# A second attention with keys on partitions: column maxima and sums by GpSimd in place of turned probabilities

## What is computed

```python
def _attention(q, k, v):
    ...
        s = jnp.einsum('bqhgd,bkhd->bhgqk', qi, k, preferred_element_type=jnp.float32)
        w = jax.nn.softmax(s, axis=-1).astype(v.dtype)
        return jnp.einsum('bhgqk,bkhd->bqhgd', w, v)
...
    q = _rope(_rmsnorm(_heads(p, OFF_Q, N_Q_HEADS), q_norm_g[l]), cos, sin) * q_scale
    attn = _attention(q, jnp.concatenate([k, kc], axis=1), jnp.concatenate([v, vc], axis=1))
...
    y_a = (attn * jax.nn.silu(z_a)) @ w_pa
```

## Time and profile before

| quantity | value |
|---|---|
| median of three runs | 2207.98 us |
| span of the profiled execution | 2206.3 us |
| TensorE matmul busy | 2197.4 us, 100% |
| VectorE busy | 1509.1 us, 68% |
| ScalarE busy | 1066.9 us, 48% |
| GpSimd busy | 63.1 us, 3% |
| mean granted TensorE clock | 0.999 |
| HBM | 215 GB/s over the span |

### The profile page before, as it was taken

How to read it: one execution, slowest core, us unless ns; L and a number is a source line. 1 busy time by engine, 2 the same in 40 slices (tenths; PEclk the granted TensorE clock), 3 DMA queues, 4 the chain that set the end, 5 groups by cost and what they waited for, 6 DMA issues and landing times.

```text
span 2206.3 us, 37987 instructions
## 1 busy us (share of the span) xinstructions
PE 2197.4 (100%) x16122; PEld 2068.7 (94%) x16122; DVE 1509.1 (68%) x1910; ACT 1066.9 (48%) x1418; POOL 63.1 (3%) x72
## 2 busy tenths in 40 slices
PE   9999999999999999999999999999999999999998
PEld 9999999999999889989988988998889999999987
DVE  7789588888889657544554555555766656577776
ACT  5444445544444546444443543444656555444443
POOL 1000000000000000000000000000100000010001
PEclk9999999999999999999999999999999999999999
DMA  8876676788787755656656666656664445678784
GB/s 275 241 225 209 192 247 221 228 281 258 256 278 264 241 182 182 195 194 194 192 195 195 183 202 203 197 186 207 235 196 148 135 144 172 216 264 294 251 281 156
DMA packets 248034, 475.00 MB, mean 215 GB/s; under 512 B 21526, under 2 KB 26000, under 8 KB 247096
## 3 DMA queue, kind: packets, MB, share of 16 engines
q1 hardware_dynamic: 243032, 454.40, 64.7%
q0 software_dynamic: 4832, 18.16, 2.5%
HBM read 468.30 MB, written 5.78 MB: 215 GB/s over the span
## 4 chain that ended last, share of the span: by engine, by line
PE 99%; issue 0%; DVE 0%; ACT 0%; POOLq 0%; POOL 0%; DVEq 0%
PE ps L888 21%; PE ps L889 21%; PE ps L890 21%; PE ps L881 11%; PE ps L882 11%; PE ps L883 11%; PE ps L805 1%; PE ps L705 1%; PE ps L794 0%; PE ps L674 0%; PE ps L902 0%; PE ps L717 0%; PE ps L784 0%; PE ps L785 0%; PE ps L783 0%
## 5 line engine op out<-in xcount | busy, mean ns | idle before, releaser
L888 PE MATMUL ps<-op0h,whiW 128*128 128x256 f32 x3376 | 936.8, 277 | 0.0
L890 PE MATMUL ps<-op0h,wloW 128*128 128x256 f32 x3376 | 932.3, 276 | 0.0
L889 PE MATMUL ps<-op0l,whiW 128*128 128x256 f32 x3376 | 932.2, 276 | 0.0
L1279 DVE TENSOR_TENSOR wloW<-raw,whiW 128x1024 fp32r<-128x1024 f32 (+1 forms) x503 | 611.0, 1227 | 339.0 <-ACT whiW L935 336.9
L935 ACT ACTIVATE whiW<-raw 128x1024 fp32r<-128x1024 f32 (+1 forms) x504 | 529.0, 1058 | 581.1 <-PE ps L890 482.8
L888 PEld LDWEIGHTS ps<-op0h,whiW 128*128 128x128 f32 x3376 | 633.7, 188 | 2.2 <-issue 1.6
L889 PEld LDWEIGHTS ps<-op0l,whiW 128*128 128x128 f32 x3376 | 633.8, 188 | 0.5
L890 PEld LDWEIGHTS ps<-op0h,wloW 128*128 128x128 f32 x3376 | 633.7, 188 | 0.0
L1279 DVE TENSOR_TENSOR wloT<-raw,whiT 128x1024 fp32r<-128x1024 f32 (+1 forms) x264 | 317.4, 1211 | 249.5 <-ACT whiT L935 248.0
L935 ACT ACTIVATE whiT<-raw 128x1024 fp32r<-128x1024 f32 (+1 forms) x264 | 273.7, 1046 | 291.0 <-PE ps L883 243.0
L881 PE MATMUL ps<-whiT,op1h 128*128 128x512 f32 x640 | 249.2, 389 | 0.0
(11 more groups left out here) (308 smaller groups left out, 2070.2 us busy)
## 6 DMA issues: line engine op xcount, KB each, us to landing
raw<-in_w_in SPq DMA_DIRECT2D x256, 512.0 KB, 4.4
raw<-in_w_up SPq DMA_DIRECT2D x128, 512.0 KB, 3.7
raw<-in_w_down SPq DMA_DIRECT2D x128, 512.0 KB, 4.0
raw<-in_w_ada SPq DMA_DIRECT2D x96, 512.0 KB, 4.7
raw<-in_w_gate SPq DMA_DIRECT2D x96, 512.0 KB, 4.8
raw<-in_w_out SPq DMA_DIRECT2D x64, 512.0 KB, 5.1
raw<-in_w_branch SPq DMA_DIRECT2D x48, 512.0 KB, 4.9
raw<-in_w_proj_a SPq DMA_DIRECT2D x24, 512.0 KB, 5.7
```

The costliest lines, as they stand in the source:

```text
L888: pe.matmul(o, wh, xh[:, ka, :], start=first and m % 2 == 0, stop=False, skip_group_check=True)
L889: pe.matmul(o, wh, xl[:, ka, :], start=False, stop=False, skip_group_check=True)
L890: mm = pe.matmul(o, wl, xh[:, ka, :], start=False, stop=last, skip_group_check=True)
L1279: v.tensor_tensor(wlo[job.mode][q % NSPL][:, :, 0:job.n], x, h.bitcast(F32), ALU.subtract).then_inc(s_lo, 1)
```

## The change

Scores are computed the other way round: 128 keys are stationary, the 256 queries of a head move, so the scores stand in four tiles of 128 keys by 256 queries. ScalarE copies them to a buffer `keyed[h % 2]` (128x1024, in place of tmp0 to tmp3). VectorE takes the maximum of the four tiles (128x256), GpSimd all-reduces the maxima of a pair of heads over partitions (`peaks2`, 128x512), VectorE subtracts them, ScalarE takes the exponential. `values2` reads these unnormalised values directly, with 256 moving columns. GpSimd adds the four tiles of each head and all-reduces the sums (`totals2`); VectorE takes the reciprocal of 128x512 and multiplies it with the gates (`softmax2_share`), and gates the values with that. Both heads' values go to bank 4. `turn2` and `softmax2_scale` are gone. The pairs stand 11, 11, 11, 17 and 11 chunks apart. `TURN_QK` names other banks for the turning of queries and keys.

```diff
+TURN_QK = ((6, 7), (5, 7), (5, 7), (5, 7), (5, 4))
...
-        heads2 = [of["za0"].first + 6, of["qq1"].first + 5, of["za1"].end, of["zb"].first + 1, of["ga0"].first + 3, of["ga0"].first + 10]
+        pairs2 = [of["za0"].first + i for i in (6, 17, 28, 39, 56, 67)]
         for i in range(6):
-            q = heads2[i]
+            q = pairs2[i]
             for h in (2 * i, 2 * i + 1):
                 side(pe_at, q, "scores2", h)
+                side(act_at, q + 1, "scores2", h)
                 side(dve_at, q + 1, "softmax2_max", h)
-                side(act_at, q + 1, "softmax2_exp", h)
-                side(dve_at, q + 1, "softmax2_scale", h)
-                side(pe_at, q + 3, "turn2", h)
-                side(act_at, q + 4, "turn2", h)
+                side(dve_at, q + 4, "softmax2_less", h)
+                side(act_at, q + 5, "softmax2_exp", h)
                 side(pe_at, q + 6, "values2", h)
-                side(dve_at, q + 7, "values2", h)
-                side(act_at, q + 7, "values2", h)
+            side(dve_at, q + 9, "softmax2_share", i)
+            for h in (2 * i, 2 * i + 1):
+                side(dve_at, q + 9, "values2", h)
+                side(act_at, q + 9, "values2", h)
...
+            def peaks2(i):
+                pool.wait_ge(s_max2, 2 * i + 2)
+                pool.partition_all_reduce(peak[:, :, :], peak[:, :, :], 128, bass.bass_isa.ReduceOp.max).then_inc(s_peak2, 1)
+
+            def totals2(i):
+                if i:
+                    pool.wait_ge(s_atv, 2 * i)
+                for e in range(2):
+                    p, o = keyed[e], total[:, e, :]
+                    pool.wait_ge(s_exp2, 2 * i + e + 1)
+                    pool.tensor_tensor(o, p[:, 0, :], p[:, 1, :], ALU.add).then_inc(s_sum2, 1)
+                    for st in (2, 3):
+                        pool.wait_ge(s_sum2, 6 * i + 3 * e + st - 1)
+                        pool.tensor_tensor(o, o, p[:, st, :], ALU.add).then_inc(s_sum2, 1)
+                pool.wait_ge(s_sum2, 6 * i + 6)
+                pool.partition_all_reduce(total[:, :, :], total[:, :, :], 128, bass.bass_isa.ReduceOp.add).then_inc(s_total2, 1)
...
-            for name in ("k", "qq0", "qq1", "qq2"):
-                rstd(name, 0)
-                rstd(name, 1)
+            rstd("k", 0)
+            rstd("k", 1)
+            rstd("qq0", 0)
+            rstd("qq0", 1)
+            peaks2(0)
+            totals2(0)
+            rstd("qq1", 0)
+            rstd("qq1", 1)
+            for i in range(1, 4):
+                peaks2(i)
+                totals2(i)
+            rstd("qq2", 0)
+            rstd("qq2", 1)
+            for i in range(4, 6):
+                peaks2(i)
+                totals2(i)
...
             def scores2(h):
...
                 if h >= 2:
-                    pe.wait_ge(s_att, h - 1)
-                    pe.wait_ge(s_trr2, 2 * h - 2)
...
+                    pe.wait_ge(s_scr2, h - 1)
+                    if e == 0:
+                        pe.wait_ge(s_atv, h)
+                qh, ql = qt[:, h, :], qtl[h // 4][:, h % 4, :]
+                for st in range(4):
+                    keys, ps = slice(128 * (st % 2), 128 * (st % 2) + 128), bank[4 + 2 * e + st // 2][:, 256 * (st % 2):256 * (st % 2) + 256]
+                    kh, kl = ((ktx, ktxl), (ktch, ktcl))[st // 2]
+                    pe.matmul(ps, kh[:, kv, keys], qh, start=True, stop=False)
+                    pe.matmul(ps, kh[:, kv, keys], ql, start=False, stop=False)
+                    mm = pe.matmul(ps, kl[:, kv, keys], qh, start=False, stop=True)
+                mm.then_inc(s_sc2, 1)
...
+                pe.wait_ge(s_exp2, h + 1)
+                for st in range(4):
+                    vv = vx if st < 2 else vc
+                    mm = pe.matmul(bank[4][:, 256 * e:256 * e + 256], vv[:, st % 2, 128 * kv:128 * kv + 128], keyed[e][:, st, :],
+                                   start=st == 0, stop=st == 3)
...
+            def scores2(h):
+                e = h % 2
+                if h >= 2:
+                    act.wait_ge(s_att, h - 1)
+                act.wait_ge(s_sc2, h + 1)
+                for i in range(2):
+                    op = act.activation(keyed[e][:, 2 * i:2 * i + 2, :], half(bank[4 + 2 * e + i]), ACT.Copy)
+                op.then_inc(s_scr2, 1)
+
             def softmax2_exp(h):
...
+                p = keyed[h % 2]
+                act.wait_ge(s_less2, h + 1)
+                act.activation(p[:, :, :], p[:, :, :], ACT.Exp, scale=ATT_SCALE).then_inc(s_exp2, 1)
...
             def softmax2_max(h):
...
+                v.wait_ge(s_scr2, h + 1)
+                v.tensor_reduce(peak[:, e, :], keyed[e][:, :, :].rearrange("p s t -> p t s"), AX, ALU.max).then_inc(s_max2, 1)
+
+            def softmax2_less(h):
+                e, p = h % 2, keyed[h % 2]
+                v.wait_ge(s_peak2, h // 2 + 1)
+                v.tensor_tensor(p[:, :, :], p[:, :, :], peak[:, e, :].unsqueeze(1).broadcast_to([128, 4, 256]), ALU.subtract).then_inc(s_less2, 1)
+
+            def softmax2_share(i):
...
+                v.wait_ge(s_total2, i + 1)
+                v.reciprocal(total[:, :, :], total[:, :, :]).then_inc(own.sem, own.up())
+                v.wait_ge(own.sem, own.n)
+                v.tensor_tensor(total[:, :, :], total[:, :, :], zs[:, 2 * i:2 * i + 2, :], ALU.mult).then_inc(s_share2, 1)
+                v.wait_ge(s_share2, i + 1)
...
             def values2(h):
...
                 v.wait_ge(s_av2, h + 1)
-                v.tensor_tensor(tm[:, 0:256], bank[4 + 2 * (h % 2)][:, 0:256], zs[:, h, :], ALU.mult).then_inc(s_atv, 1)
+                v.tensor_tensor(x, bank[4][:, 256 * e:256 * e + 256], total[:, e, :], ALU.mult).then_inc(s_atv, 1)
```

More of the change, by code:

```diff
@@ L380, in program @@
         cdt = bg("cdt", [128, 2, 128], 60)
+        keyed = [at(f"keyed{e}", [128, 4, 256], tmp_at + 4096 * e) for e in range(2)]
+        peak, total = at("peak", [128, 2, 256], tmp_at + 10240), bg("total", [128, 2, 256], 69)
         rot = [bg(f"rot{i}", [128, 512], 61 + 2 * i) for i in range(4)]
@@ L797, in values2 @@
+                mm.then_inc(s_sc2, 1)
             def values2(h):
                 e, kv = h % 2, h // 3
[L799 to L806, removed]
+                if h == 0:
+                    pe.wait_ge(s_pair[of["vx"].pair], of["vx"].after)
@@ L1034, in split_kc @@
                 act.activation(ktch, ktc[:, :, :], ACT.Copy).then_inc(s_kch, 1)
-            def softmax2_exp(h):
[L1037 to L1050, removed]
+            def scores2(h):
[6 more added lines that the diff above has]
+                op.then_inc(s_scr2, 1)
+            def softmax2_exp(h):
+                p = keyed[h % 2]
+                act.wait_ge(s_less2, h + 1)
+                act.activation(p[:, :, :], p[:, :, :], ACT.Exp, scale=ATT_SCALE).then_inc(s_exp2, 1)
             def values2(h):
                 act.wait_ge(s_atv, h + 1)
-                act.activation(op1h[:, h, :], tmp[4 + h % 2][:, 0:256], ACT.Copy).then_inc(s_ahi, 1)
+                act.activation(op1h[:, h, :], keyed[h % 2][:, 0, :], ACT.Copy).then_inc(s_ahi, 1)
             def fourier_t(g):
@@ L1205, in ep_gate2 @@
                     act.wait_ge(s_qkt, 10)
+                    if which == "b" and c == 1:
+                        act.wait_ge(s_atv, 12)
                 for m in range(4):
@@ L1544, in softmax2_max @@
             def softmax2_max(h):
[L1545 to L1550, removed]
+                e = h % 2
+                v.wait_ge(s_scr2, h + 1)
[5 more added lines that the diff above has]
+            def softmax2_share(i):
+                job = of[f"za{i // 2}"]
+                if i % 2 == 0:
+                    v.wait_ge(s_pair[job.pair], job.after)
+                v.wait_ge(s_total2, i + 1)
[3 more added lines that the diff above has]
+                v.wait_ge(s_share2, i + 1)
             def turn_qk(s, tt):
@@ L1560, in split_kc @@
                 v.tensor_tensor(ktcl[:, :, :], ktc[:, :, :], ktch.bitcast(F32), ALU.subtract).then_inc(s_kcl, 1)
[L1562 to L1568, removed]
-            def values2(h):
[L1571 to L1578, removed]
+            def values2(h):
+                e = h % 2
+                x = keyed[e][:, 0, :]
                 v.wait_ge(s_av2, h + 1)
-                v.tensor_tensor(tm[:, 0:256], bank[4 + 2 * (h % 2)][:, 0:256], zs[:, h, :], ALU.mult).then_inc(s_atv, 1)
+                v.tensor_tensor(x, bank[4][:, 256 * e:256 * e + 256], total[:, e, :], ALU.mult).then_inc(s_atv, 1)
                 v.wait_ge(s_ahi, h + 1)
-                v.tensor_tensor(op1l[:, h, :], tm[:, 0:256], op1h[:, h, :].bitcast(F32), ALU.subtract).then_inc(s_att, 1)
+                v.tensor_tensor(op1l[:, h, :], x, op1h[:, h, :].bitcast(F32), ALU.subtract).then_inc(s_att, 1)
             def fourier_d(g):
```

47 lines of the change are left out of this document (17 added, 30 removed).

## The result

The changed kernel takes 2253.97 us, the median of four runs (2250.46 to 2254.76), where the kernel before takes 2208.02: ratio 1.0204, 95% interval 1.0192 to 1.0217, slower by 46 us. The execution that was profiled is the fastest of the four, 2250.46 us, with a span of 2248.5 us, 42.2 more than the span before.

What follows compares the result with a forecast made beforehand. TensorE, busy practically the whole span, was taken as the bound. Waits of 3 x 6.2 + 6.4 + 5.0 + 11.4 + 14 = 55.4 us minus 11.3 removed make +44.1 on 2207.98: 2252 us, range 2206 to 2280.

Steps and rivals of the forecast that it cites:

- What goes away: TensorE: transposes of probabilities gone, 10.5 us, value matmuls 0.8 us less, scores cost the same; gain 11.3 us without waits.
- Maxima: VectorE, start of a pair's chain: maximum over 1024 values, 2 x 0.68 us; a strided read could cost twice that.
- All-reduce: GpSimd, 128x512, for a pair's maxima and again for its sums: mean 3.7 us each.
- Way back: GpSimd: changing its code from the all-reduce to ordinary adds, 8.4 us, hidden in a plain pair with 1 us of cover.
- Way forth: GpSimd: changing its code to the all-reduce's between additions and the all-reduce of sums, 8.4 us, bounds 0 and 9.4.
- rival 2: Cheap change of GpSimd's code, dear reciprocal: 21 us of waits minus 11.3, 2218 us; chance 0.13.
- Reciprocal: VectorE, 512 columns between all-reduced sums and gating: taken as 5.0 us, between 0.49 and 5.6.
- The sum of waits: TensorE: 6.2 us after pairs 0, 2 and 4, 6.4 at pair 5, 5.0 and 11.4 at pair 1, 14 near qq2; 55.4.
- Pair 1: rstd of qq1 between GpSimd's all-reduces delays pair 1's maxima all-reduce to 14 us behind its scores; pair 2's scores wait 11.4 us.
- late weights of chunks 19 to 21: Scaling and rotating of qq1 hold up these weights and the exponentials: 5.0 us of TensorE waiting.
- rival 3: TensorE's clock falls too, in waits of 6 us and more: 2.6 us for each of seven, 2270 us; chance 0.13.
- Rival 1: All hidden, faster: free change to the all-reduce's code, reciprocal near 0.5 us, gating within 33.5 us; 2196.7 us; chance 0.17.

Runs made afterwards that it cites:

- switch_after_adds: adds_on_vector plus one single-column GpSimd addition per pair, placed behind VectorE's six additions and before the all-reduce of the sums: 2250.25 us, ratio 1.0191.
- adds_on_vector: Changed kernel with the six additions of each pair moved from GpSimd to VectorE: 2213.25 us, ratio 1.0024 to the kernel before.
- no_reciprocal: Changed kernel with the reciprocal of 128x512 left out, gates multiplied with the sums themselves: 2224.2 us, ratio 1.0075 to the kernel before.
- adds_spread_v7: adds_spread with the value matmuls of pair 5 one chunk later: 2204.11 us, ratio 0.9984 to the kernel before.
- adds_spread: adds_on_vector with maxima by three comparisons and gating at q + 8, 8, 8, 11, 9 and 13 for the six pairs: 2205.24 us, ratio 0.9987.
- late_share: Changed kernel with reciprocal, gating and low part of pairs 3 and 5 at position q+12 instead of q+9: 2244.67 us, ratio 1.0165.

## Why the prediction was right, and where its terms were off

The mechanism was read right: each pair's chain through GpSimd and VectorE is longer than TensorE's slack. The time, 2254 against 2252 us, is nearer than the terms were, by luck. Step by step:

- **What goes away** was right. The value matmuls of a pair take 3.45 us, scores keep their 0.120 us, the transposes are gone.
- **Maxima** were too cheap. The strided reduction of 128x1024 takes 2.02 us, not 1.4; the upper bound had it (twice). For the four pairs whose additions waited for the exponentials it did not count. For pairs 1 and 3 it did: there the additions waited for the way back, which starts behind the all-reduce of the maxima, and two heads are some 1.2 us of that chain.
- **All-reduce** of the maxima: 1.8 to 2.7 us, mean 2.38, instead of 3.7; of the sums 3.29.
- **Way back** 7.0 to 8.4 us where it is exposed, as predicted. The six additions took 5.6 to 6.5 us with hand-overs instead of 4.8.
- **Way forth** was the term known least, 0 to 9.4, taken as 8.4. It is 6.3 on the mean. The choice of the nearest row over 0 made most of the forecast's loss: with 0, rival 2 still had the kernel slower, by 10 us instead of 44. switch_after_adds shows that it was the right mechanism. The 6 us of the Trainium skill, GPSIMD Engine Reference, "Instruction dispatch", are nearer to this term.
- **Reciprocal** 3.35 us. I took 5.0, too long. The estimate from the Trainium skill (VectorE: DVE Perf Modes, "First, the fixed hardware budget") was 4.3, too long as well.
- **The sum of waits** is therefore 38.2 us and not 55.4. Plain pairs 3.4, 4.8 and 3.1 where I had 6.2 each, pair 5 5.0 and 0.9 before its values where I had 6.4, pair 1 6.5 where I had 16.4. At qq2 14.5 against 14: the order (scaling queued behind the rstd behind the sums, the reciprocal behind the rotation) was read right, but the number is partly luck. Pair 3's all-reduce of the maxima started 9.5 us behind its scores where I had 3, and the shorter all-reduces, changes of code and reciprocal gave that back.
- **Pair 1** is the step whose reading failed, not only its size. I had the code ready for its maxima 12 us behind its scores, 55 us behind pair 0's; the rstds of qq1 were through at 1699.0, some 5 us earlier than I had, and the way forth is 2 us shorter. So its all-reduce waited for VectorE's maxima, 10.97 us, and not for "issue". The late weights of chunks 19 to 21 do not show either in the changed kernel, where TensorE came out of the wait at half its clock; in adds_on_vector, where it came there at the full clock, they do, with 2.2 us in two gaps.
- **The clock** was a rival (3), priced at 18 us and left out of the sum. It happened in each of the six waits above 3 us, where the rival had spoken of 6 us and more, and cost some 14 us; in adds_on_vector even a wait of 1.9 us had 3.4 us of lower clock behind it. I had the waits 17 us too long and the clock at nothing, 14 us too short, and that these two errors cancelled is luck. Forecast and rival 3 together are what took place.

Rival 1 (all hidden) needed a free way forth and a reciprocal of 0.5 us; no_reciprocal, which comes near the second (no reciprocal at all), still lost 16 us, and rival 1 is out. Rival 2 needed a free way forth; adds_on_vector is near what it described, at 2213 us against its 2218.

## What to carry to other kernels

Before a step is put on GpSimd, count how often its queue goes from an all-reduce to ordinary instructions and back: here 7 to 9 us one way and about 6 us the other, hidden where it can run beside another engine's work, paid in full where it starts behind the last thing it waits for. One single-column addition per pair cost 31 us more in the wrong place than in the right one. Where TensorE had never waited, 38 us of waits cost another 14 us at the lower clock here, while the waits of 1.1 to 1.5 us in adds_spread_v7 cost none (in adds_spread two of 1.5 us, 2.6 us apart, still had 3.4 us of lower clock behind them). So a chain should be shorter than its slack, not about as long.

## What the runs showed that I had not expected

The reciprocal of 128x512 takes 3.35 us, 6.5 ns a column, 3346 to 3355 ns in its six cases.

All-reduces of 128x512 are not of one length: 1.8, 2.7 or 4.9 us for the maxima. In the changed kernel pair 1's took 2.66 us, and in late_share, where everything up to there is the same program and it started equally long, 0.14 us, behind VectorE's maxima, 4.93 us:

```profile
1710.09 4.93 POOL L558 PARTITION_ALL_REDUCE peak<-peak  x1 [10.96 <-DVE peak L1567]
...
1726.52 3.28 POOL L569 TENSOR_TENSOR total<-total,keyed 128x256 f32<-128x256 f32 x2
1736.62 3.25 POOL L571 PARTITION_ALL_REDUCE total<-total  x1 [6.82 <-issue]
```

Beside it VectorE ran three low parts, which read two operands in SBUF, first in the changed kernel, then in late_share:

```profile
1709.73 4.33 DVE L1300 TENSOR_TENSOR wloW<-raw,whiW 128x1024 fp32r<-128x1024 f32 x3
1709.87 3.48 DVE L1300 TENSOR_TENSOR wloW<-raw,whiW 128x1024 fp32r<-128x1024 f32 x3
```

One side pays each time. In all 11 traces with this all-reduce it is one of these two pairs of lengths: in six VectorE takes 4.33 us and the all-reduce 2.66, in five VectorE some 3.5 us and the all-reduce 4.93. Likewise two additions took 3.28 us in late_share and 1.56 in the changed kernel, beside the low parts too. The Trainium skill, SBUF — State Buffer, "Who interferes with whom", has the port that such an instruction shares with GpSimd as an exclusive lock. The lengths fit that, but no run here took the low parts away, so it stays argued. It moved pair 1's sums by 4.3 us from one execution to the next, and may be why the changed kernel's runs spread over 4 us where those of before spread over 1.
